# An expert layer with its gather and spread moved from DMA onto TensorE in a decoder kernel on one core

## Chip, cores and metric

One Trainium2 chip, one core. The metric is the device time of one execution in microseconds (us), all data in float32.

## What is computed

The reference runs one decoder layer over 256 tokens with 16 learned meta tokens in front (272 rows of width D = 2048). A combined input projection feeds three mixers (HGRN2, mLSTM, Mamba-2), an output projection `w_out` (2048 x 2048) adds their result to the residual `h`, and then comes the part that matters here:

```python
u = rmsnorm(h, norm_ffn_w)                        # rows of 2048
g = softmax(u @ w_group + b_group)                # 4 groups, the best one is taken
e = (u @ w_router[group] + b_router[group])       # 8 experts of that group, the best two are taken
out[t] = sum over the two: weight * (silu(u[t] @ w1[e]) * (u[t] @ w3[e])) @ w2[e]
result = rmsnorm(h + out, final_norm_w)[:, 16:]   # the meta rows are dropped
```

There are 32 experts; `w1` and `w3` are 2048 x 512, `w2` is 512 x 2048, so an expert has 3 x 4.19 MB and all of them 402.7 MB. Of the 272 rows each picks two experts, 17 rows to an expert on average. With the reference's inputs the busiest expert gets 28.

## The kernel before

**Projections.** `ring` is a buffer of six slots of 2 MB. The input projection (52 column tiles of 128) and the output projection (16 tiles, u = 52 to 67) stream their weights in chunks of two tiles, chunk c into slot c % 2 (SyncE, L435). A chunk is asked for when all tiles of chunk c - 2 are finished (`in_tile`). In the output projection TensorE computes each tile as 16 matmuls over all 272 rows (`mixed`, L1278 to L1284); a float32 matmul is two instructions in the trace. The first four tiles are computed in three parts each (L1491 to L1507), since their inputs are finished one group after the other (`hg_gated`, `z_done`, `norm_done`). VectorE adds each tile to `hT` (L1171), the residual with features on the partitions. ScalarE squares it (L782) and scales it by the norm weight (L783).

**Routing.** After the last tile TensorE computes the logits (L1519), the sums of squares (L1524) and turns the normalised rows to token order (L1537), and ScalarE writes them to DRAM (`tokens_normed`, L800). VectorE picks groups and experts (`routing`, L284 to L376): up to `chosen` (L327) it finds who goes where; TensorE ranks the rows of each expert (L1541 to L1546); then six rounds with a matmul each (L1551) make, for every expert, the list of its rows, as indices for an indirect DMA. Last, `hT` is turned to token order (L1561) for the final sum.

**Experts.** A pass handles up to 64 rows of one expert (`CAP` = 64); experts with more rows would get further passes, their number is read from `ov_n`. GpSimd gathers the rows from DRAM by an indirect DMA (`gather`, L539), TensorE turns them (L1569), and for `w1` and `w3` runs 32 matmuls of 64 columns by 512 (`up`, L1573): `w1` is used on PSUM partitions 0 to 63 and `w3` on 64 to 127, so that two column groups of the array are in use at a time. ScalarE copies the hidden rows out (L820), TensorE turns them (L1590), ScalarE and VectorE gate them, TensorE runs 16 matmuls for `w2` (`down`, L1593), both halves of D side by side in the array. ScalarE and VectorE weight the result (L830, L1192), and GpSimd scatters it to DRAM (`expert_rows`, `scatter`, L550).

**Order.** Each engine has its program written out by hand. On TensorE an iteration is: up(i), turn rows of i + 1, down(i - 1), turn hidden of i (L1619 to L1623). SyncE loads an expert's weights as six transfers of 2 MB, each into a slot of the ring once the matmuls that read the slot last are done (L446, L456, L459, L472). The four transfers of `w1` and `w3` of expert 0 go out behind the last chunk of `w_out`, the two of `w2` when `w_out` is finished (`in_ev`).

**End.** After the last scatter the rows come back from DRAM (L488), VectorE adds them to `h2` in four additions (L1222, L1224), then come the sum of squares, the root (through Ln and Exp, with table loads), the scaling (L1228) and the transfer out (L491).

Of the kernel before, what the change touches and what calls it, by code (L numbers as in the profile page):

```python
# [28 lines left out]
def hymba_moe_layer(nc, x, meta_tokens, hg_lb_logits, norm_mix_w, w_in, hg_norm_w, ml_b_i, ml_b_f,  # L29
# [4 lines left out]
    i32 = mybir.dt.int32  # L34
# [23 lines left out]
    CAP = 64  # L58
    NB = -(-T // CAP)
    NOV = (2 * T) // (CAP + 1)  # L60
    NC_ = NB * NE

# [31 lines left out]
    with ctx:  # L94
# [6 lines left out]
        ring = sb("ring", [P, NSLOT * SLOT])  # L101
        hT = sb("hT", [P, KD, T])
        uT = sb("uT", [P, KD, T])
        proj = sb("proj", [P, NP_, T])
        pflat = proj[:, :, :].rearrange("p a t -> p (a t)")
# [49 lines left out]
        fss = sb("fss", [P, 2])  # L155
        frs = sb("frs", [P, 2])
# [24 lines left out]
        moff = [0]  # L181

        def mo(n):
            moff[0] += n
            assert moff[0] <= NP_ * T
            return pflat[:, moff[0] - n:moff[0]]


        sqk = proj[:, X0:X0 + 8, :]
        sqa = proj[:, B0, :]  # L190
        lgT = proj[:, B0 + 1, :]
        u2 = mo(NT * D).rearrange("p (a d) -> p a d", a=NT)
        h2 = pflat[:, 0:2 * D].rearrange("p (a d) -> p a d", a=2)
        xs = mo(1024)
        xsT = mo(1024).rearrange("p (c h s) -> p c h s", c=8, h=2)
        hs = mo(512)
        ssb = mo(KF * CAP).rearrange("p (k s) -> p k s", k=KF)
        hTb = mo(KF * CAP).rearrange("p (k s) -> p k s", k=KF)
        ysb = mo(1024)
        fw = uT[:, 0:8, :].rearrange("p k t -> p (k t)")[:, 0:D]  # L200
        hid_ps = pb[3][:, :].rearrange("p (k c) -> p k c", k=KF)

        rat = [moff[0]]

        def ro(n):
            rat[0] += n
            assert rat[0] <= NP_ * T
            return pflat[:, rat[0] - n:rat[0]]

        idx_base = sb("idx_base", [P, 3, NC_])  # L210
        idx_x = sb("idx_x", [P, NC_], i32)
        idx_y = sb("idx_y", [P, NC_], i32)
        ov_x = sb("ov_x", [P, NOV], i32)
        ov_y = sb("ov_y", [P, NOV], i32)
        ov_w = sb("ov_w", [P, NOV])
        ov_e = sb("ov_e", [P, NOV], i32)
        ov_n = sb("ov_n", [P, 1], i32)
        xcol = sb("xcol", [P, 1], i32)
        ycol = sb("ycol", [P, 1], i32)

        u2d = nc.dram_tensor("tokens_normed", (2 * T, 1024), f32, kind="Internal").ap()
        yd = nc.dram_tensor("expert_rows", (4 * T, 1024), f32, kind="Internal").ap()
# [12 lines left out]
            "lg_T rs2 iotas gmax pairs ranks gmax_e rhs_used rhs_ready idx_ready ov_ready gatew_in "  # L235
            "par_in routerw_in in_a in_b in_ev h_ps y_ps y_out f_done out_sem pool_steps "
            "ident_ready consts pool_waited xT_ps col_x xs_in col_y y_act y_dve ys_out y_free "
            "u2_out act_steps conv_done params_zeroed rms_ready gate_cols_in lb_diff lb_exp "
            "alog_exp gf_ready gcols_ready li_ready fd_x fd_tanh fd_e em_t em_exp in_tile conv_acc "
            "xv_T xv_ev e_ready e_exp sq_ready sum_ready rs_ready ssm_gated hsig hg_gate hlin hln z_gate "  # L240
            "hv_T hv_ev lv_d lv_e ml_e ml_exp ml_o ml_abs ml_h mo_gate hg_done sq_acc sq2 "
            "u2T_ready sum2 t_ps t_ev h2_ps h2_ev fw_in xT_ev h_ev hT_ps silu_ev f_sum f_rs "
            "dve_steps x_T x_ev par_T par_ev diag_ready R_ready uT_ready g_rows g_col g_colev "
            "cb_ready cb_ev bc_ready y_ready pt_ready y_ev lv_ps lv_w lvd_ps lv_ev ho_ps ho_ev "
            "ml_ps ml_pt norm_done lg_ready row_ps row_ev hlin_q hg_gated z_done lg_ev xT_ev2 hT_ready"
# [6 lines left out]


        LG = GRP + NE
        io_e = ro(NE)
        io_s = ro(P)
        io_t = ro(2 * NT).rearrange("p (a j) -> p a j", j=2)
        io_c = ro(NC_ - NE)
# [25 lines left out]
        def routing(dve, V, step):  # L284
# [14 lines left out]
            for a in range(NT):  # L299
                last = V.max(mg[:, a, :], g8[:, a, :])  # L300
# [1362 lines left out]
```

## Time and profile before

| | |
|---|---|
| median of 3 runs | 1681.1 us (1680.99 to 1681.78) |
| the profiled execution | 1683.12 us, its span 1681.4 us |
| TensorE matmul busy | 1452.1 us, 86% of the span |
| VectorE, ScalarE, GpSimd busy | 285.2, 250.5, 88.9 us |
| granted TensorE clock, mean | 0.928 of full |
| read from HBM | 498.79 MB, mean 309 GB/s with the 21.10 MB written |

The page slices the span into 40 parts of 42 us; a matmul's busy time includes its way through the array, so a busy TensorE need not be at its peak. The span runs from the first to the last instruction; the device time lies 1.7 us above it.

### The profile page before, as it was taken

To read this page: it belongs to the slowest core of one execution; us is meant where nothing else is said; L and a number is where in the kernel's file an instruction comes from. 1 tells how busy PE (TensorE), PEld (TensorE's weight loads), DVE (VectorE), ACT (ScalarE), POOL (GpSimd) and SP (SyncE) were. 2 spreads that over 40 slices of the span, in tenths; PEclk is the share of its full clock that TensorE was granted. 3 is DMA by queue.
4 is the path that set the end of the run, shared out by engine and by line. 5 is a ranking of instruction groups with operands and counts; after the bars stand their busy time and mean duration, and the time that the engine had idled before them with its cause. 6 is when DMAs were issued, how large, how long until landed. Compare 5 with 4: busy or idle time off the path is not lost.

```text
span 1681.4 us, 16119 instructions
## 1 busy us (share of the span) xinstructions
PE 1452.1 (86%) x6416; PEld 806.2 (48%) x6416; DVE 285.2 (17%) x714; ACT 250.5 (15%) x396; POOL 88.9 (5%) x172
## 2 busy tenths in 40 slices
PE   6999999999998997888878888788788788887881
PEld 3888888777886784433323323223233232232230
DVE  4312542341211014121000000000000000000003
ACT  2112413112150012210000100000001001000002
POOL 2000000000000000010000100100000001000000
PEclk9999999999999999898989989989889899898896
DMA  6343354334332565699999999999999999999994
GB/s 160 100 150 100 101 130 128 101 101 133 118 100 86 164 241 213 248 426 427 428 427 426 427 425 423 423 411 412 424 414 417 424 416 425 418 414 421 415 409 171
DMA packets 125982, 495.83 MB, mean 295 GB/s; under 512 B 27988, under 2 KB 97752, under 8 KB 99928
## 3 DMA queue, kind: packets, MB, share of 16 engines
q1 hardware_dynamic: 115536, 482.98, 72.4%
q0 software_dynamic: 9216, 8.94, 1.5%
q10 hardware_dynamic: 1192, 3.37, 0.6%
q8 instruction: 27, 0.44, 0.1%
q14 instruction: 11, 0.09, 0.0%
HBM read 498.79 MB, written 21.10 MB: 309 GB/s over the span
## 4 chain that ended last, share of the span: by engine, by line
PE 57%; DMA 39%; DVE 1%; ACT 1%; SPq 1%; issue 1%; POOLq 0%; ACTq 0%; DVEq 0%
DMA ring<-in_moe_w_dram 37%; PE bank L1239 24%; PE bank L1582 18%; PE bank L1282 7%; PE bank L1321 1%; DMA ring<-in_w_out_dram 1%; PE bank L1299 1%; PE bank L1250 1%; SPq L446 1%; PE bank L1293 1%; PE bank L1603 1%; PE bank L1267 1%; DMA ring<-in_x_dram 1%; PE bank L1371 1%; PE bank L1519 0%
## 5 line engine op out<-in xcount | busy, mean ns | idle before, releaser
L1582 PE MATMUL bank<-ring,proj 128*64 128x512 f32 x2048 | 530.4, 677 | 160.4 <-DMA ring<-in_moe_w_dram 159.5
L1582 PEld LDWEIGHTS bank<-ring,proj 128*64 128x64 f32 x2048 | 183.0, 156 | 487.1 <-issue 486.0
L1239 PE MATMUL bank<-uT,ring 128*128 128x272 f32 x1664 | 390.3, 394 | 0.0
L1239 PEld LDWEIGHTS bank<-uT,ring 128*128 128x128 f32 x1664 | 313.5, 190 | 64.4 <-issue 1.5
L1603 PE MATMUL bank<-ring,proj 128*64 128x512 f32 x1024 | 227.0, 595 | 1.3 <-DVE proj L1187 0.9
L1603 PEld LDWEIGHTS bank<-ring,proj 128*64 128x64 f32 x1024 | 71.1, 137 | 135.0 <-issue 132.3
L1182 DVE COPY proj<-bank 128x512 f32<-128x512 f32 x32 | 22.1, 692 | 665.4 <-PE bank L1569 665.4
L820 ACT ACTIVATE proj<-bank 128x512 f32<-128x512 f32 x32 | 34.5, 1079 | 674.2 <-PE bank L1582 674.2
L1282 PE MATMUL bank<-proj,ring 128*128 128x272 f32 x512 | 122.8, 404 | 9.2 <-DMA ring<-in_w_out_dram 9.2
L1282 PEld LDWEIGHTS bank<-proj,ring 128*128 128x128 f32 x512 | 100.4, 197 | 31.4 <-DMA ring<-in_w_out_dram 10.0
L640 ACT ACTIVATE proj<-bank 128x272 f32<-128x272 f32 x52 | 20.7, 397 | 296.1 <-PE bank L1239 296.1
L1192 DVE TENSOR_SCALAR proj<-bank,idx_base 128x512 f32<-128x512 f32 x32 | 24.0, 751 | 228.1 <-PE bank L1603 228.1
L830 ACT ACTIVATE proj<-bank,idx_base 128x512 f32<-128x512 f32 x32 | 22.0, 687 | 210.1 <-PE bank L1603 210.1
L557 POOL DMA_INDIRECT expert_rows<-proj,ycol x32 | 32.5, 1015 | 221.7 <-DVE proj L1192 203.6
L543 POOL COPY xcol<-idx_x 128x1 int32 (+1 forms) x32 | 5.8, 183 | 661.9 <-PE bank L1569 630.6
L1569 PEld LDWEIGHTS bank<-ident,proj 128*128 128x128 f32 x256 | 27.4, 141 | 26.3 <-issue 26.3
L1569 PE MATMUL bank<-ident,proj 128*128 128x128 f32 x256 | 34.9, 280 | 1.0 <-ACT proj L809 1.0
L546 POOL DMA_INDIRECT proj<-tokens_normed,xcol x32 | 33.3, 1041 | 25.7 <-POOL xcol L543 25.7
L523 POOL IOTA proj<- 128x32 f32 x1 | 0.2, 158 | 628.7 <-DVE hT L1171 628.7
L1590 PEld LDWEIGHTS bank<-ident,proj 128*128 128x128 f32 x128 | 13.4, 140 | 25.5 <-issue 25.1
L1171 DVE TENSOR_TENSOR hT<-hT,bank 128x272 f32 x16 | 7.0, 438 | 106.9 <-PE bank L1282 106.9
L782 ACT ACTIVATE proj<-hT 128x272 f32<-128x272 f32 x16 | 6.9, 430 | 119.3 <-DVE hT L1171 119.3
(294 smaller groups left out, 706.4 us busy)
## 6 DMA issues: line engine op xcount, KB each, us to landing
ring<-in_moe_w_dram SPq DMA_DIRECT2D x192, 2048.0 KB, 20.3
ring<-in_w_in_dram SPq DMA_DIRECT2D x26, 2048.0 KB, 8.2
ring<-in_w_out_dram SPq DMA_DIRECT2D x8, 2048.0 KB, 8.1
ring<-expert_rows SPq DMA_DIRECT2D x4, 1024.0 KB, 8.2
tokens_normed<-proj ACTq DMA_DIRECT2D x2, 1024.0 KB, 3.9
out_dram<-ring SPq DMA_DIRECT2D x2, 1024.0 KB, 3.9
ring<-in_x_dram SPq DMA_DIRECT2D x1, 1024.0 KB, 8.3
uT<-in_final_norm_w_dram ACTq DMA_DIRECT2D x1, 1024.0 KB, 4.6
```

The lines of the kernel that those rows point to most:

```text
L546: V.indirect_dma_start(out=xs, out_offset=None, in_=u2d[:, :], in_offset=bass.IndirectOffsetOnAxis(ap=xcol[:, 0:1], axis=0), bounds_check= ...
L557: V.indirect_dma_start(out=yd[:, :], out_offset=bass.IndirectOffsetOnAxis(ap=ycol[:, 0:1], axis=0), in_=ysb, in_offset=None, bounds_check= ...
L640: V.activation(proj[:, TILES[u], :], pb[u % 4][:, 0:T], func).then_inc(s["in_ev"], 1)
L820: V.activation(hs.rearrange("t (j k p) -> t j p k", j=2, k=2), pb[2][:, :].rearrange("t (j p k) -> t j p k", j=2, k=2), ACT.Copy).then_inc ...
L830: V.activation(ysb[:, 0:512], pb[4][:, :], ACT.Copy, scale=wcol).then_inc(s["y_act"], 1)
L1182: V.tensor_copy(xsT[:, 4:8, :, :].rearrange("p c h s -> p (c h s)"), pb[1][:, :]).then_inc(s["xT_ev2"], 1)
L1192: V.tensor_scalar(ysb[:, 512:1024], pb[5][:, :], wcol, None, ALU.mult).then_inc(s["y_dve"], 1)
L1239: last = V.matmul(outs, a, b, start=start and j == 0, stop=stop and j == n - 1)
L1282: last = V.matmul(pb[u % 4][:, 0:T], wchunk(c % 2)[:, k, u % 2 * P:(u % 2 + 1) * P], proj[:, MIXED[k], :], start=k == 0, stop=k == 7)
L1569: last = V.transpose(pb[c // 4][:, (c % 4) * P:(c % 4 + 1) * P], xs[:, c * P:(c + 1) * P], ident[:, :])
L1582: last = V.matmul(pb[2][64 * g:64 * g + 64, :], xsT[:, c, part, :], w[:, c, :], start=part + c == 0, stop=part == 1 and c == 7)
L1603: last = V.matmul(pb[4 + d][64 * g:64 * g + 64, :], hTb[:, k, :], w[:, k % 2, g * 1024 + d * 512:g * 1024 + (d + 1) * 512], start=k == 0, ...
```

## The change

The routing covers the 256 real tokens only. A pass has 32 places (`CAP` = 32) and four column groups (`QR` = 4): group g computes the quarter g of the contraction (for `w1`, `w3`) or of D (for `w2`). Gather and scatter through DRAM are gone. For a pass, VectorE makes a one-hot matrix from ranks (`tokens_hot`), TensorE multiplies it with the token rows `u2` (`tokens`), ScalarE copies out, TensorE turns. The four partial hidden results are summed by the product with `selq` in `turn_hidden`. The expert's output is spread back to the token rows by 8 matmuls of 32 rows of contraction each (`combine`), with weighted one-hot matrices turned by `spread`, and VectorE adds each of the 8 to `h2` (`sums`). The weights go into four slots of 4 MB, one matrix each, in two transfers; the logits, the squares and the turn to token order are made tile by tile in the output projection (`by_rows`), which now covers 256 columns. Its first two tiles, not four, are made in parts. The final norm works on pieces of 512 as they come.

```diff
-    CAP = 64
+    NA = SEQ // P
+    CAP = 32
+    QR = P // CAP
+        E_AT = (2 * SLOT, 4 * SLOT, 0, RING + KD * T)
+        def halves(j, e, r):
+            if r < 2:
+                v = (moe_w1, moe_w3)[r][0, bass.ds(e, 1), :, :].rearrange("e (p h k) f -> p h (e k f)", p=P, h=2)
+            else:
+                v = moe_w2[0, bass.ds(e, 1), :, :].rearrange("e (p h k) d -> p h (e k d)", p=P, h=2)
+            return [(eslot(j)[:, h * SLOT:(h + 1) * SLOT], v[:, h, :]) for h in range(2)]
...
+                if 2 * c == NIN + 2:
+                    sp.wait_ge(s["norm_done"], 1)
+                    for dst, src in halves(0, 0, 0):
+                        sp.dma_start(dst, src).then_inc(m_in[0], 16)
+                if 2 * c == NIN + 6:
+                    for dst, src in halves(1, 0, 1):
+                        sp.dma_start(dst, src).then_inc(m_in[1], 16)
+            sp.wait_ge(s["in_tile"], NIN + NOUT)
+            for dst, src in halves(2, 0, 2):
+                sp.dma_start(dst, src).then_inc(m_in[2], 16)
+            sp.wait_ge(s["t_ps"], 4 * NA)
+            sp.wait_ge(s["lg_ready"], 1)
+            for dst, src in halves(3, 1, 0):
+                sp.dma_start(dst, src).then_inc(m_in[3], 16)
+            used = (s["h1_ps"], s["h3_ps"], s["y_ps"])
+            for m in range(4, 16):
+                sp.wait_ge(used[(m - 4) % 3], (m - 4) // 3 + 1)
+                for dst, src in halves(m % 4, m // 3, m % 3):
+                    sp.dma_start(dst, src).then_inc(m_in[m % 4], 16)
...
+            for g in range(4):
+                for a in range(NA):
+                    pool.wait_ge(s["t_ev"], NA * g + a + 1)
+                    V.tensor_tensor(u2[:, a, :].rearrange("t (c p) -> t c p", p=P)[:, :, 32 * g:32 * (g + 1)],
+                                    h2[:, a, g * 512:(g + 1) * 512].rearrange("t (q c) -> t c q", c=16),
+                                    nwrow[:, g * 512:(g + 1) * 512].rearrange("t (q c) -> t c q", c=16),
+                                    ALU.mult).then_inc(s["u2_ev"], 1)
...
+            act.wait_ge(s["ov_ready"], 1)
+            act.dma_start(fw, final_norm_w.partition_broadcast(P)).then_inc(s["fw_in"], 16)
...
+            def sums(n, first=False):
+                for j in range(8):
+                    a, d = j // 4, j % 4
+                    dve.wait_ge(s["cb_ps"], n * 8 + (j + 1))
+                    V.tensor_tensor(h2[:, a, d * 512:(d + 1) * 512], h2[:, a, d * 512:(d + 1) * 512],
+                                    pb[6 + j % 2][:, :], ALU.add).then_inc(s["y_acc"], 1)
...
-                    last = V.matmul(pb[u % 4][:, 0:T], wchunk(c % 2)[:, k, u % 2 * P:(u % 2 + 1) * P],
-                                    proj[:, MIXED[k], :], start=k == 0, stop=k == 7)
+                    last = V.matmul(pb[u % 4][:, 0:SEQ], wchunk(c % 2)[:, k, u % 2 * P:(u % 2 + 1) * P],
+                                    proj[:, MIXED[k], NM:T], start=k == 0, stop=k == 7)
...
+            def by_rows(k):
+                pe.wait_ge(s["in_ev"], 4 + NIN + k + 1)
+                if k % 4 == 0 and k:
+                    pe.wait_ge(s["t_ev"], NA * (k // 4))
+                for a in range(NA):
+                    last = V.transpose(pb[5 + a][:, (k % 4) * P:(k % 4 + 1) * P],
+                                       hT[:, k, NM + a * P:NM + (a + 1) * P], ident[:, :])
+                    if k % 4 == 3:
+                        last.then_inc(s["t_ps"], 1)
+                for a in range(NA):
+                    last = V.matmul(pb[(4, 7)[a]][:, 0:LG], hT[:, k, NM + a * P:NM + (a + 1) * P], wr[:, k, :],
+                                    start=k == 0, stop=k == KD - 1)
+            def tokens(n):
+                pe.wait_ge(s["oh_ready"], n + 1)
+                for a in range(NA):
+                    for g in range(QR):
+                        last = V.matmul(pb[0][CAP * g:CAP * (g + 1), :], oh[:, a, :], u2[:, a, g * 512:(g + 1) * 512],
+                                        start=a == 0, stop=a == NA - 1)
+            def up(n, slots, counts):
+                pe.wait_ge(s["xT_ev"], n + 1)
+                for r in range(2):
+                    pe.wait_ge(m_in[slots[r]], counts[r])
+                    w = eslot(slots[r]).rearrange("p (k f) -> p k f", f=FE)
+                    for j in range(4):
+                        for g in range(QR):
+                            last = V.matmul(pb[2 + r][CAP * g:CAP * (g + 1), :], xsT[:, j, g, :], w[:, 4 * g + j, :],
+                                            start=j == 0, stop=j == 3)
+                    last.then_inc((s["h1_ps"], s["h3_ps"])[r], 1)
+            def turn_hidden(n):
+                for r, hs in ((0, hs1), (1, hs3)):
+                    pe.wait_ge((s["h1_ev"], s["h3_ev"])[r], n + 1)
+                    for k in range(KF):
+                        last = V.matmul(pb[4][:, (r * KF + k) * CAP:(r * KF + k + 1) * CAP], hs[:, k * P:(k + 1) * P],
+                                        selq[:, :], start=True, stop=True)
+            def down(n, slot_, count):
+                pe.wait_ge(s["hT_ready"], n + 1)
+                pe.wait_ge(m_in[slot_], count)
+                for k in range(KF):
+                    for g in range(QR):
+                        last = V.matmul(pb[5][CAP * g:CAP * (g + 1), :], hTb[:, k * CAP:(k + 1) * CAP],
+                                        w[:, k, g * 512:(g + 1) * 512], start=k == 0, stop=k == KF - 1)
+            def combine(n, first=False):
+                for j in range(8):
+                    a, g = j // 4, j % 4
+                    if not first or j >= 2:
+                        pe.wait_ge(s["y_acc"], n * 8 + (j - 1))
+                    V.matmul(pb[6 + j % 2][:, :], wT[CAP * g:CAP * (g + 1), a * P:(a + 1) * P],
+                             ysb[CAP * g:CAP * (g + 1), :], start=True, stop=True).then_inc(s["cb_ps"], 1)
+            def one(n, at, last=False, first=False):
+                up(n, [at[0][0], at[1][0]], [at[0][1], at[1][1]])
+                if not last:
+                    tokens(n + 1)
+                turn_hidden(n)
+                if not last:
+                    turn_tokens(n + 1)
+                if not first:
+                    combine(n - 1)
+                spread(n)
+                down(n, *at[2])
```

## Rows read from the trace of the kernel before

**Rows 1.** The page: tenths in 40 slices, and one DMA queue (packets, MB, share)

```profile
PEclk9999999999999999898989989989889899898896
DMA  6343354334332565699999999999999999999994
GB/s 160 100 150 100 101 130 128 101 101 133 118 100 86 164 241 213 248 426 427 428 427 426 427 425 423 423 411 412 424 414 417 424 416 425 418 414 421 415 409 171
...
q0 software_dynamic: 9216, 8.94, 1.5%
```

**Rows 2.** Windows: length, then busy us of PE, PEld, DVE, ACT, POOL, clock, DMA share, GB/s

```profile
640.00:680.00 40.00, 30.09 (x148) 18.84 (x145) 18.29 (x95) 15.60 (x28) 2.83 (x7) 0.83 0.43 164
...
750.00:780.00 30.00, 24.96 (x114) 9.45 (x112) 4.76 (x21) 2.57 (x4) 2.45 (x4) 0.94 1.01 427
...
1110.00:1140.00 30.00, 24.75 (x106) 9.15 (x107) 1.86 (x3) 2.52 (x4) 2.44 (x4) 0.89 0.98 408
```

**Rows 3.** The chain that ended last, in one expert: start, us, what

```profile
796.36 20.17 DMA ring<-in_moe_w_dram
816.52 0.14 issue
816.66 9.78 PE bank L1582 x31
```

**Rows 4.** The expert weights' transfers: one line's issues, then SyncE's timeline (start, us)

```profile
L456 SPq MOVE ring<-in_moe_w_dram x30: 29/29/37, 724.2 to 1607.5; - x30
...
610.09 3.30 SPq L446 DMA_DIRECT2D ring<-in_moe_w_dram  x4
...
689.40 0.80 SPq L446 DMA_DIRECT2D ring<-in_moe_w_dram  x2
```

**Rows 5.** Timeline of the output projection: start, us, then idle time before and its releaser

```profile
507.04 3.83 PE L1282 MATMUL bank<-proj,ring 128*128 128x272 f32 x16
507.24 102.81 SPq L435 DMA_DIRECT2D ring<-in_w_out_dram  x7
...
507.67 1.50 DVE L1162 TENSOR_TENSOR proj<-proj,ring 128x272 f32<-128x272 f32 x4 [1.36 <-ACT proj L640]
...
515.55 28.99 PE L1282 MATMUL bank<-proj,ring 128*128 128x272 f32 x112 [4.67 <-DMA ring<-in_w_out_dram]
...
549.03 89.95 PE L1282 MATMUL bank<-proj,ring 128*128 128x272 f32 x384 [4.50 <-DMA ring<-in_w_out_dram]
```

**Rows 6.** Timeline of the routing: start, us, then idle time before

```profile
649.19 0.57 DVE L294 SCALAR_TENSOR_TENSOR proj<-bank,rs,brow 128x36 f32<-128x36 f32 x3 [1.99 <-ACT rs L789]
...
653.82 0.26 DVE L327 TENSOR_TENSOR proj<-proj 128x96 f32<-128x96 f32 x1
...
655.92 0.97 PE L1239 MATMUL bank<-proj,ones 128*128 128x32 f32 x6
...
682.32 10.09 PE L1582 MATMUL bank<-ring,proj 128*64 128x512 f32 x46 [0.83 <-ACT proj L815]
```

**Rows 7.** Groups by shape: count, busy us and mean ns, idle before and releaser

```profile
L1192 DVE TENSOR_SCALAR proj<-bank,idx_base 128x512 f32<-128x512 f32 x32 | 24.0, 751 | 228.1 <-PE bank L1603 228.1
...
L815 ACT ACTIVATE proj<-bank 128x512 f32<-128x512 f32 x32 | 19.1, 597 | 1.4 <-PE bank L1569 1.4
...
L820 ACT ACTIVATE proj<-bank 128x512 f32<-128x512 f32 x32 | 34.5, 1079 | 674.2 <-PE bank L1582 674.2
```

**Rows 8.** Timeline of TensorE inside one expert

```profile
1072.15 7.09 PE L1582 MATMUL bank<-ring,proj 128*64 128x512 f32 x32 [1.99 <-DMA ring<-in_moe_w_dram]
...
1078.18 0.17 PEld L1582 LDWEIGHTS bank<-ring,proj 128*64 128x64 f32 x2 [0.26 <-issue]
1079.17 0.85 PEld L1569 LDWEIGHTS bank<-ident,proj 128*128 128x128 f32 x8 [0.81 <-issue]
```

**Rows 9.** The chain that ended last, its last part: start, us, what

```profile
1625.51 19.70 DMA ring<-in_moe_w_dram
...
1650.59 2.64 DMA expert_rows<-proj,ycol
```

**Rows 10.** Timeline of the end

```profile
1662.20 2.29 DVE L1224 TENSOR_TENSOR proj<-proj,ring 128x2048 f32<-128x2048 f32 x1 [0.21 <-DMA ring<-expert_rows]
...
1672.15 5.27 SPq L491 DMA_DIRECT2D out_dram<-ring  x2
```

More of the change, by code:

```diff
@@ L473, in _ @@
+            for m in range(88, 3 * NE):
+                sp.wait_ge(used[(m - 4) % 3], (m - 4) // 3 + 1)
+                for dst, src in halves(m % 4, m // 3, m % 3):
+                    sp.dma_start(dst, src).then_inc(m_in[m % 4], 16)
+            sp.wait_ge(s["y_ps"], NE - 1)
             sp.wait_ge(s["ov_ready"], 1)
@@ L862, in _ @@
+            for a in range(NA):
+                act.wait_ge(s["f_rs"], a + 1)
+                act.wait_ge(s["f_g"], 4 * a + 2)
+                V.activation(fout[:, a, 0:1024], fout[:, a, 0:1024], ACT.Copy, scale=frs[:, a:a + 1]).then_inc(
+                    s["f_act"], 1)
         @block.vector
@@ new lines, in _ @@
+            by_rows(NOUT - 1)
+            pe.wait_ge(s["pairs"], 1)
+            for a in range(NA):
+                product(pb[7][:, a * NE:(a + 1) * NE],
+                        [(ones[:, 0:P], chosen[:, j, :]) for j in range(a)] + [(before[:, :], chosen[:, a, :])])
+            product(pb[7][:, NA * NE:(NA + 1) * NE],
+                    [(ones[:, 0:P], chosen[:, a, :]) for a in range(NA)]).then_inc(s["ranks"], 1)
+            def tokens(n):
+                pe.wait_ge(s["oh_ready"], n + 1)
+                for a in range(NA):
+                    for g in range(QR):
+                        last = V.matmul(pb[0][CAP * g:CAP * (g + 1), :], oh[:, a, :], u2[:, a, g * 512:(g + 1) * 512],
+                                        start=a == 0, stop=a == NA - 1)
+                last.then_inc(s["xs_ps"], 1)
@@ new lines, in _ @@
+            pe.wait_ge(s["u2_ev"], 4 * NA)
+            tokens(0)
+            turn_tokens(0)
+            one(0, places(0), first=True)
+            up(1, [places(1)[0][0], places(1)[1][0]], [places(1)[0][1], places(1)[1][1]])
+            tokens(2)
+            turn_hidden(1)
+            turn_tokens(2)
+            combine(0, first=True)
+            spread(1)
+            down(1, *places(1)[2])
+            for n in (2, 3, 4):
+                one(n, places(n))
+            with pe.Fori(1, 7) as i:
+                for q in range(1, 5):
+                    one(i * 4 + q, [(j, i * 96 + c) for j, c in places(q)])
@@ L1628, in _ @@
+            for n in range(29, NE):
+                one(n, places(n), last=n == NE - 1)
             pe.wait_ge(s["ov_ready"], 1)
             count = pe.value_load(ov_n[0:1, 0:1], min_val=0, max_val=NOV)
+            combine(NE - 1)
             with pe.If(count > 0):
                 with pe.Fori(0, count) as i:
-                    turn_rows(i + NE)
-                    up(i + NE, (1, 0))
+                    tokens(i + NE)
+                    turn_tokens(i + NE)
+                    up(i + NE, [0, 1], [i * 32 + (32 * (3 * NE // 4) + 32)] * 2)
```

773 lines of the change are left out of this document (312 added, 461 removed).

## Prediction, made before the changed kernel was run

> **What bounds the kernel now.** The page first: from the eighteenth slice to the last but one the DMA row reads 9 and the traffic 411 to 428 GB/s, where the mixers moved 86 to 248 [rows 1]. The windows confirm it: DMA share 1.01, TensorE busy 24.96 of 30 us [rows 2]. The chain of waits then shows one pattern per expert: a transfer of 20.17 us, 9.78 us of matmuls of L1582, and the next transfer [rows 3]. A transfer of 2 MB takes that long because it stands behind others, so the chain's matmul pieces are no second bound: transfers queue without a hole. From 724.2 to 1607.5 us the first slot of `w2` was refilled 30 times, so an expert takes 883.3 / 29 = 30.46 us [rows 4]. It moves 12.58 MB of weights and 8.94 / 32 = 0.28 MB of gathered and scattered rows [rows 1], together 422 GB/s. The transfers of expert 0 are the only ones made ahead; the next is issued at 689.40 [rows 4], 50.4 us after the last matmul of `w_out` (549.03 + 89.95 = 638.98) [rows 5]. Six transfers of about 5 us each cannot fill that, and the window of the routing shows a DMA share of 0.43 [rows 2]. The last weights land at 1625.51 + 19.70 = 1645.2 [rows 9], and 36.2 us of end follow. The span is thus 638.98 + 50.4 + 955.8 + 36.2 = 1681.4 us.
>
> **The change, part by part.** I build its span anew and compare it with 1681.4.
>
> *Output projection.* 384 instructions of 272 columns take 89.95 us, 0.234 us each [rows 5]; with 256 columns 0.2205, a tile of 32 takes 7.06 us. Sixteen take 113.0 us from 507.04. The pieces of 4 tiles made TensorE wait 4.67 and 4.50 us for chunks 27 and 28 [rows 5]. Now two tiles fill the time from 507.04 to 521.2. Chunk 27 lands at about 515.5, chunk 28 is asked for at 521.2 behind the first 4 MB of expert 0, issued when the group norm ends at 509.2 (507.67 + 1.50) [rows 5], and lands before 530, needed at 536. Both stalls go, and what comes late next is nothing, since a chunk is used in 15 us and a 4 MB transfer with a chunk behind takes about 18, with one chunk of slack. `by_rows` adds 2 turns and 4 short matmul instructions per tile. Eight weight loads of 128 columns take 0.85 us, 0.106 each [rows 8]; by that 0.64 us a tile, bounded from above by 0.2 each. Fourteen lie before the last tile's end: 9.0 us. The end E is 507.04 + 113.0 + 9.0 = 629.0. ScalarE's squares and copies (4 of about 0.6 to 0.8 us for each fourth tile), VectorE's scaling of `wr` (about 1 us, after 509.2, needed at 521) and the first GpSimd multiplies lie beside the tiles; their cover is over 28 us per four tiles.
>
> *Routing.* After E: addition 0.6, `by_rows` 1.0, two squares 1.6, sum, root and reciprocal 0.9, choosing 4.5 (649.19 to 654.08 for three row tiles), ranks 1.5, last small steps 1.0 [rows 6], tokens 2.1, copy 0.8, turn 0.7, copy 0.8 [rows 7]: `up` of expert 0 starts at E + 15.5, against 682.32 - 638.98 = 43.3 now [rows 6]. GpSimd's last two multiplies must be done by E + 11. VectorE adds 2048 elements of two inputs in 2.29 us [rows 10], 0.57 for 512; GpSimd may be three times slower and still has 3 us for each.
>
> *When DMA runs dry.* Two matrices have landed by E; the third goes out at E + 0.2, the fourth at E + 1.6. Chunk 27, alone, came 8.3 us after its issue (507.24 to 515.55) [rows 5] against 5 us in the stream, so 3.3 us of start. Both are in at E + 23. The first slot is freed by the first half of `up`, at E + 19.0, at half clock E + 22.5. So the hole of the routing closes; I take 0 and keep 0 to 5.
>
> *The stream.* From E on, 94 matrices of 4.194 MB. At 422 GB/s each takes 9.93 us: 933.4 us. A stretch without the GpSimd queue isn't in the trace; the best window is 427, one without disturbance on it was 408, though the gathers were alike in both [rows 2]. So I credit the missing 0.28 MB and nothing more; 427 gives 923, 408 gives 966. The final norm's weights, 1 MB across all partitions, now go out beside the last `w2`: 2.5 us. The last weights land at D = 629.0 + 0.2 + 3.3 + 933.4 + 2.5 = 1568.4.
>
> *TensorE must keep up*: 29.8 us per expert. Two column groups give 7.09 / 32 = 0.222 us per instruction of 512 columns [rows 8]; one would give 0.2342 x 512 / 272 = 0.441 [rows 5], so two ran side by side in full. With four I take p = 0.111 for the 64 + 16 + 32 instructions of `up`, `tokens` and `down`: 12.4 us; the upper bound is 0.222. `combine` has two banks: matmul 0.88, hand-over 0.3 to 0.4, addition 0.75 [rows 7], two in flight: 1.0 each, 8.0 us. Turns: 22 loads of 0.106, 2.3 us. At a change from column groups to the whole array the next loads come 0.99 us after the last pair's, which otherwise follow each other by 0.43 [rows 8]: 0.56 us, four times 2.2. Sum 24.9, and up to 2.7 more at the half clock after an idle stretch (9.78 against 7.09) [rows 3, 8]: 27.6. It fits, hidden behind the transfers. VectorE has some 9.5 us per expert (8 additions of 0.75), ScalarE 3.5. Four slots of 4 MB let a matrix be used up to 29 us after it landed before SyncE's next wait starves the queue; the matrix of `w2` is used about 10 us late.
>
> In the Trainium skill, TensorE: Matmul & The Clock Gate, the section on measured speedup gives 3.07 for four row tiles rather than 4. By that p would be 0.139 and the sum 28.0, still under 29.8. The Trainium skill's TensorEngine Tiling, Key Properties, says that changing the tiling mode drains TensorE, which the 0.56 us bears out; it asks for no other number.
>
> *The end.* `w3` of expert 31 is in 12.4 us before D. Half an `up` 3.5, copy and turn 2.3, `combine` of expert 30 8.0, spread 0.8: `down` starts at D + 2.1, ends D + 5.9. Copy 0.8, `combine` 8.6, then norm 3 and 1 for GpSimd's lag (no row shows its multiply): D + 19.3. The 512 KB out take about 3.5; now 1 MB leaves at 1677.1 and ends at 1681.4 [rows 10]. Scatter (2.64 us) [rows 9], read-back, the long additions and the table loads in between are gone. End: 22.8 against 36.2.
>
> **Sum.** 1568.4 + 22.8 = 1591.2, 90.2 under 1681.4. The profiled execution is at 1683.12, 2.0 above the median of 1681.1, so the median becomes 1681.1 - 90.2 = 1590.9. By parts: output projection -10.0, from there to the start of the stream -46.9 (50.4 to 3.5), more weights after it but faster ones -19.9 (955.8 to 935.9), end -13.4.
>
> **Rivals.**
> - *TensorE becomes the bound, slower.* Four column groups give no more than two. For: every instruction of L1582 and L1603 uses two, no row uses four. Against: two scaled fully. With p = 0.222 an expert takes 37.3 us; from 644.5 on 32 of them and 17 us give 1855. It is slower than now above 31.9 us an expert, which is p above 0.173.
> - *TensorE is the bound, but mildly*, p 0.155 to 0.173, or `combine` handing over more slowly: 30 to 31.9 us an expert, 1605 to 1675, say 1650. The margin of 2 to 5 us speaks for it.
> - *The routing still leaves the DMA dry*, as it does now: the first slot free at E + 50, 27 us of hole: 1618. GpSimd's multiplies or a wait chain I read too kindly would do it.
> - *The weights come at 408 GB/s throughout*, since a matrix is now read in strides of 32 KB: 1624.
> - *It doesn't do what it says*: with 32 places instead of 64 there are further passes, over 30 us each. The busiest expert has 28 rows, so none.
>
> **Chances.** Forecast 0.73; mildly bound 0.08; dry start 0.07; slow weights 0.05; slower 0.06; further passes 0.01. The range 1573 (427 GB/s and an end 6 us shorter) to 1625 holds the forecast, the dry start and the slow weights. About 0.2% is what a measurement can tell from no change. Faster 0.93, same 0.01, slower 0.06.
>
> **What would show it.** Right: `up` of expert 0 at 640 to 650, no window after 630 with a DMA share under 0.95, refills of one slot 39.7 us apart (four matrices), `up` in about 7 us for 64 instructions, 20 to 25 us from the last landing to the end. Wrong: in the chain, `combine` or L1582's successor without transfers between; `up` at 14 us; a hole in DMA before 680.

## The result and the profile after

The changed kernel takes 1595.8 us (1590.2 to 1596.0, 4 runs) against 1681.2 for the kernel before on the same chip: a ratio of 0.948, 95% interval 0.946 to 0.950. The forecast was 1591 with a range of 1573 to 1625. The profiled execution has a span of 1593.7 us, 87.7 under the 1681.4 of before.

The page of the changed kernel, to be read beside [rows 1]: the span, TensorE, then clock, DMA share and traffic in 40 slices of 40 us.

```profile
span 1593.7 us, 18575 instructions
...
PE 1461.9 (92%) x7715; PEld 793.2 (50%) x7715; DVE 448.8 (28%) x1033; ACT 314.2 (20%) x470; POOL 36.5 (2%) x59
...
PEclk9999999999999999878867878778778778788786
DMA  6335253333444833899999999999999999999992
GB/s 169 106 106 159 84 135 106 106 106 106 130 134 165 316 127 144 359 428 426 428 428 428 428 428 429 429 428 428 428 429 428 428 429 429 428 428 428 429 426 112
```

The weights are still what the time waits for: the DMA row has a 9 in every slice from the eighteenth to the last but one, and the traffic there is now an even 426 to 429 GB/s where before had 409 to 428. The queue of the indirect DMAs is gone from the page. The clock row is new: mostly 7 and 8 where before had 8 and 9.

Windows of the changed kernel (columns as in [rows 2]):

```profile
630.00:660.00 30.00, 20.02 (x122) 7.74 (x122) 11.28 (x48) 6.98 (x11) 3.76 (x2) 0.66 0.81 338
...
648.00:650.00 2.00, 2.00 (x16) 0.52 (x12) 0.00 (x0) 0.32 (x1) 0.00 (x0) 0.50 0.31 131
650.00:652.00 2.00, 2.00 (x12) 0.39 (x8) 0.00 (x0) 0.00 (x0) 0.00 (x0) 0.50 0.00 0
652.00:654.00 2.00, 2.00 (x20) 0.56 (x16) 0.00 (x0) 0.32 (x1) 0.00 (x0) 0.76 0.00 0
654.00:656.00 2.00, 2.00 (x24) 0.48 (x16) 0.00 (x0) 0.28 (x1) 0.00 (x0) 1.00 0.79 197
...
1110.00:1140.00 30.00, 26.15 (x162) 9.27 (x158) 7.51 (x15) 5.23 (x7) 0.00 (x0) 0.83 1.01 428
```

A hole is left in the transfers, from 648.6 to 654.4. By the DMA shares it is 2 x 0.69 + 4 + 2 x 0.21 = 5.8 us. After it there is none, and TensorE has under 4 us of 30 to spare. At 428 GB/s a matrix of 4.194 MB takes 9.80 us.

The timeline from the last tile of the output projection to the first refill, against [rows 5, 6]:

```profile
620.55 7.15 PE L1256 MATMUL bank<-big 128*128 128x256 f32 x32
...
637.40 0.63 PE L1213 MATMUL bank<-big,before 128*128 128x32 f32 x2 [8.37 <-DVE big L322]
...
640.92 3.64 PE L1516 MATMUL bank<-big 128*32 128x512 f32 x16 [1.18 <-DVE big L1100]
...
645.27 1.12 PE L1523 MATMUL bank<-ident,big 128*128 128x128 f32 x4 [0.71 <-ACT big L729]
...
647.07 9.97 PE L1533 MATMUL bank<-big 128*32 128x512 f32 x64 [0.69 <-ACT big L733]
...
653.68 4.24 SPq L426 DMA_DIRECT2D big<-in_moe_w_dram  x4
```

The projection ends at E = 627.70 (620.55 + 7.15), both of its stalls are gone, and `up` of expert 0 starts at E + 19.4. TensorE was idle for 8.4 us ahead of the ranks and stays at half clock until 653. So the first half of `up` takes 6.6 us instead of 3.64.

One expert inside the loop on TensorE, against [rows 8]; L1533 is `up`, L1568 `combine`, L1557 `down`:

```profile
991.65 3.64 PE L1533 MATMUL bank<-big 128*32 128x512 f32 x32 [2.69 <-DMA big<-in_moe_w_dram]
995.10 1.90 PE L1516 MATMUL bank<-big 128*32 128x512 f32 x16
...
999.31 1.13 PE L1568 MATMUL bank<-big 32*128 32x512 f32 x4
1001.21 2.67 PE L1568 MATMUL bank<-big 32*128 32x512 f32 x4 [0.77 <-DVE big L1127]
...
1010.12 5.92 PE L1557 MATMUL bank<-big 128*32 128x512 f32 x32
1015.87 3.61 PE L1533 MATMUL bank<-big 128*32 128x512 f32 x32
```

Four column groups run side by side in full: 3.64 / 32 = 0.114 us per instruction of 512 columns. In `combine` two matmuls lie on different row groups and share their time (their four instructions take 1.13 us together), then wait for VectorE. From the second pair on a pair takes 2.67 us. The windows show a clock of 0.50 from 1002 until about 1014, so `down` takes 5.92 us for as many instructions as `up` runs in 3.6.

The timeline of the end, against [rows 9, 10]. The traffic into the chip's buffers ends at D = 1560.4, by the windows; as in the prediction, the 1 MB of the final norm's weights is part of it:

```profile
1549.57 3.64 PE L1533 MATMUL bank<-big 128*32 128x512 f32 x32 [0.77 <-DMA big<-in_moe_w_dram]
...
1557.01 8.37 PE L1568 MATMUL bank<-big 32*128 32x512 f32 x12 [0.84 <-DVE big L1127]
...
1565.93 6.20 PE L1557 MATMUL bank<-big 128*32 128x512 f32 x32
...
1574.85 10.30 POOL L514 TENSOR_TENSOR big<-big 128x512 f32<-128x512 f32 x8 [940.16 <-DVE big L1127]
...
1586.82 2.88 SPq L451 DMA_DIRECT2D out_dram<-big  x4
```

`down` of the last expert starts 5.5 us after D, when its weights are there, because `combine` of expert 30 stands ahead of it at half clock. The end takes 33.3 us.

**Where the 87.7 us came from.** Output projection 638.98 to 627.70: 11.3. From there to the stream: 50.4, now the hole of 5.8 and a remainder of 3.2, which I put down to the queue's starts and its last, partly filled microseconds: 41.4. The weights after it: 955.8, now 94 x 9.80 + 2.5 = 923.7: 32.1. The end, 36.2 to 33.3: 2.9.

### The profile page after: what moved, and what is told of

The parts are those of the page before. It is cut to its first block, busy times and chain, and to the rows that moved or that the text cites. A ratio compares the mean times of both kernels' runs of the same rounds, so it can differ in the third digit from the quotient of the medians.

```text
span 1593.7 us, 18575 instructions
## 1 busy us (share of the span) xinstructions
PE 1461.9 (92%) x7715; PEld 793.2 (50%) x7715; DVE 448.8 (28%) x1033; ACT 314.2 (20%) x470; POOL 36.5 (2%) x59
## 4 chain that ended last, share of the span: by engine, by line
PE 66%; DMA 29%; DVE 2%; ACT 1%; issue 1%; SPq 0%; ACTq 0%; DVEq 0%
DMA big<-in_moe_w_dram 29%; PE bank L1213 25%; PE bank L1568 9%; PE bank L1533 8%; PE bank L1256 7%; PE bank L1557 6%; PE bank L1516 2%; PE bank L1541 2%; DVE big L1127 1%; PE bank L1295 1%; PE bank L1273 1%; PE bank L1224 1%; PE bank L1267 1%; PE bank L1241 1%; PE bank L1548 1%; DMA big<-in_x_dram 1%
## 5 line engine op out<-in xcount | busy, mean ns | idle before, releaser
L1213 PE MATMUL bank<-big 128*128 128x272 f32 x1664 | 390.3, 394 | 0.0
L1213 PEld LDWEIGHTS bank<-big 128*128 128x128 f32 x1664 | 313.3, 190 | 64.6 <-issue 1.5
L1568 PE MATMUL bank<-big 32*128 32x512 f32 x512 | 278.7, 917 | 32.4 <-DVE big L1127 31.6
L1533 PE MATMUL bank<-big 128*32 128x512 f32 x2048 | 243.4, 619 | 61.6 <-DMA big<-in_moe_w_dram 60.9
L1127 DVE TENSOR_TENSOR big<-big,bank 128x512 f32<-128x512 f32 x256 | 169.1, 686 | 162.0 <-PE bank L1568 160.9
L1557 PE MATMUL bank<-big 128*32 128x512 f32 x1024 | 180.7, 870 | 0.0
L1533 PEld LDWEIGHTS bank<-big 128*32 128x32 f32 x2048 | 62.7, 114 | 236.2 <-issue 147.8
L1568 PEld LDWEIGHTS bank<-big 32*128 32x128 f32 x512 | 92.8, 247 | 174.0 <-DVE big L1127 164.1
L1256 PE MATMUL bank<-big 128*128 128x256 f32 x512 | 113.9, 381 | 0.0
L1256 PEld LDWEIGHTS bank<-big 128*128 128x128 f32 x512 | 96.3, 190 | 12.6
L1557 PEld LDWEIGHTS bank<-big 128*32 128x32 f32 x1024 | 40.0, 153 | 122.1 <-issue 121.9
L1541 PEld LDWEIGHTS bank<-selq,big 128*128 128x128 f32 x512 | 59.6, 191 | 26.8 <-issue 26.8
L1516 PE MATMUL bank<-big 128*32 128x512 f32 x512 | 62.4, 607 | 1.2 <-DVE big L1100 1.2
L1541 PE MATMUL bank<-selq,big 128*128 128x32 f32 x512 | 63.1, 277 | 0.0
L1516 PEld LDWEIGHTS bank<-big 128*32 128x32 f32 x512 | 16.5, 111 | 40.2 <-issue 40.2
```

Of the source, the lines that this page charges most:

```text
L1127: V.tensor_tensor(h2[:, a, d * 512:(d + 1) * 512], h2[:, a, d * 512:(d + 1) * 512], pb[6 + j % 2][:, :], ALU.add).then_inc(s["y_acc"], 1)
L1213: last = V.matmul(outs, a, b, start=start and j == 0, stop=stop and j == n - 1)
L1256: last = V.matmul(pb[u % 4][:, 0:SEQ], wchunk(c % 2)[:, k, u % 2 * P:(u % 2 + 1) * P], proj[:, MIXED[k], NM:T], start=k == 0, stop=k == 7)
L1516: last = V.matmul(pb[0][CAP * g:CAP * (g + 1), :], oh[:, a, :], u2[:, a, g * 512:(g + 1) * 512], start=a == 0, stop=a == NA - 1)
L1533: last = V.matmul(pb[2 + r][CAP * g:CAP * (g + 1), :], xsT[:, j, g, :], w[:, 4 * g + j, :], start=j == 0, stop=j == 3)
L1541: last = V.matmul(pb[4][:, (r * KF + k) * CAP:(r * KF + k + 1) * CAP], hs[:, k * P:(k + 1) * P], selq[:, :], start=True, stop=True)
```

## Experiments

In each, theory A is the one that I held, and the others are its rivals. Where no interval is given there was one run. The experiments ran on several chips, on which the kernel before took 1681.0 to 1683.4 us, and the changed kernel's own nine times lie between 1590.2 and 1596.2. So a difference of some us from 1595.8 means little by itself, and the profiles have to show where it arises.

**The half clock of the routing.** 23 spare matmuls into an unused bank where TensorE would idle:

```diff
+            def fill(n):
+                for _ in range(n):
+                    V.matmul(pb[1][:, 0:SEQ], ident[:, :], ones[:, 0:SEQ], start=True, stop=True)
+            fill(18)
```

(and 3, 1 and 1 more around `tokens` and `turn_tokens` of expert 0)

> The changed kernel with 23 spare matmuls of 256 columns on TensorE, put where it waits between the last row step of the output projection and the first expert. In the changed kernel the granted clock is 0.50 from 632 to 653 us, the first half of expert 0's up takes 6.6 us, the first refill of a slot goes out at 653.68, and no DMA runs for some 6 us before it. Theory A (the half clock makes the hole): clock 1.00 until 650, tokens of expert 0 in 1.8 us rather than 3.67, first refill at 646 to 648, no hole, total 5 to 6 us less, about 1590. Rival B (the hole is made by VectorE's chain and the copies): first refill within 2 us of 653.7, total within 1 us of the changed kernel.

1589.4 us (1589.2 to 1590.2), ratio 0.945 [0.944, 0.946], 6.4 under the changed kernel. Its window, `up` of expert 0 and its first refill:

```profile
630.00:660.00 30.00, 28.96 (x220) 15.41 (x223) 16.15 (x68) 9.40 (x14) 3.88 (x2) 1.00 0.99 416
```

```profile
643.70 7.07 PE L1538 MATMUL bank<-big 128*32 128x512 f32 x64 [0.25 <-ACT big L733]
...
647.40 4.24 SPq L426 DMA_DIRECT2D big<-in_moe_w_dram  x4
```

The clock is full, the refill comes 6.3 us earlier, and the hole is gone but for 0.4 us (a DMA share of 0.81 from 648 to 650). The span falls by as much, from 1593.7 to 1587.4: theory A.

**The half clock of the loop.** `combine` over all 128 rows, so that it adds all four quarters; what it sums is not the layer's output.

```diff
-                    V.matmul(pb[6 + j % 2][:, :], wT[CAP * g:CAP * (g + 1), a * P:(a + 1) * P],
-                             ysb[CAP * g:CAP * (g + 1), :], start=True, stop=True)
+                    V.matmul(pb[6 + j % 2][:, :], wT[:, a * P:(a + 1) * P],
+                             ysb[:, :], start=True, stop=True)
```

> The changed kernel with combine's 8 matmuls taken over all 128 rows of ysb and wT in place of 32 rows; it leaves out the choice of a quarter, so the output is another sum. In the changed kernel the clock drops to 0.50 about 2 us into combine and stays there through down. Theory A (matmuls that use a quarter of the array's rows let the clock fall): clock near 1.00 in combine and down, down in 3.6 us rather than 5 to 6, mean clock over 0.90, the end (last DMA to the end of the span) 6 to 10 us shorter, total 6 to 10 us less. Rival B (the waits between the matmuls, for VectorE's additions, let it fall): clock, down and total unchanged within 1 us.

1590.4 us (1586.3 to 1590.9), ratio 0.945 [0.943, 0.946]: 5.4 less, a little under the 6 to 10 of theory A. On TensorE, in the same expert as above and at the end, and the first refill:

```profile
1001.20 7.60 PE L1568 MATMUL bank<-big 128*128 128x512 f32 x16
...
1008.95 3.64 PE L1557 MATMUL bank<-big 128*32 128x512 f32 x32
...
1564.08 3.64 PE L1557 MATMUL bank<-big 128*32 128x512 f32 x32
1568.44 7.77 PE L1568 MATMUL bank<-big 128*128 128x512 f32 x16 [0.72 <-ACT big L746]
```

```profile
652.83 4.24 SPq L426 DMA_DIRECT2D big<-in_moe_w_dram  x4
```

The clock stays up and `down` takes 3.64 us. The saving is made at the end and not in the routing: with the first refill at 652.83 the span is 1588.3, where a second profile of the changed kernel has the refill at 652.88 and a span of 1593.1.

But two things had changed, the rows and the waits for VectorE: the page's group of this line has 1.1 us of idle time in all, where the changed kernel's has 32.4. So a last experiment kept the 32 rows and was to take the waits away, by issuing every matmul of `combine` twice:

```diff
-                    V.matmul(pb[6 + j % 2][:, :], ...).then_inc(s["cb_ps"], 1)
+                    for _ in range(2):
+                        last = V.matmul(pb[6 + j % 2][:, :], ...)
+                    last.then_inc(s["cb_ps"], 1)
```

> Each of the 8 matmuls of combine is issued twice in a row into the same bank (the second writes the same values again), still over 32 rows. In the changed kernel two of them, on different row groups, run side by side in 1.13 us and TensorE then waits 0.77 us for VectorE's additions; after that the granted clock is 0.50. The run with 128 rows took away both things at once: the few rows, and the waits (1.1 us of idle ahead of that line in the whole run, against 32.4). Theory A, the few rows lower the clock: it falls here too, in spite of TensorE having no waits, a combine takes 12 to 16 us, an expert 31 to 35 us, TensorE becomes the bound and the time is 1650 to 1750. Theory B, the waits lower the clock: a combine takes 8 to 10 us without waits of over 0.2 us, down takes 3.64 again, the granted clock in the window 1110 to 1140 is 0.89 to 0.95, the time 1587 to 1594. If the clock stays up in combine but TensorE still waits, or falls in some experts only, neither is shown.

1694.1 us, 13 more than the kernel before on its chip. From its timeline and its windows:

```profile
1095.27 1.99 PE L1569 MATMUL bank<-big 32*128 32x512 f32 x8
1098.03 12.42 PE L1569 MATMUL bank<-big 32*128 32x512 f32 x24 [0.77 <-DVE big L1127]
```

```profile
1104.00:1106.00 2.00, 2.00 (x5) 0.81 (x3) 0.76 (x2) 0.00 (x0) 0.00 (x0) 0.50 1.11 475
1106.00:1108.00 2.00, 2.00 (x5) 1.31 (x5) 0.62 (x1) 0.00 (x0) 0.00 (x0) 0.50 0.96 410
```

TensorE is busy without a gap for 12.4 us, and the clock stays at 0.50. So 32 rows of contraction hold it down, without any wait: theory A. But the run took away fewer waits than meant. The one after the first pair is left in nearly every expert (28.2 us in all), and the clock falls most often right behind it. That the fall needs no wait either is shown by two experts only. One of them:

```profile
898.39 1.97 PE L1541 MATMUL bank<-selq,big 128*128 128x32 f32 x16
900.19 0.63 PE L1523 MATMUL bank<-ident,big 128*128 128x128 f32 x4
900.76 2.84 PE L1569 MATMUL bank<-big 32*128 32x512 f32 x8
904.36 4.37 PE L1569 MATMUL bank<-big 32*128 32x512 f32 x8 [0.76 <-DVE big L1127]
```

```profile
898.00:900.00 2.00, 2.00 (x23) 1.62 (x15) 0.51 (x2) 1.45 (x2) 0.00 (x0) 1.00 1.01 434
900.00:902.00 2.00, 2.00 (x14) 1.37 (x15) 0.29 (x1) 1.31 (x3) 0.00 (x0) 0.94 0.94 401
902.00:904.00 2.00, 1.60 (x4) 0.02 (x2) 0.39 (x1) 0.00 (x0) 0.00 (x0) 0.50 1.05 451
```

The clock is down before the wait of 0.76 us begins. Nor is a wait of that length enough: in the changed kernel `up` at 991.65 follows an idle time of 2.69 us and takes 3.64 us, at full clock.

An expert of this run takes (1640.3 - 656.9) / 31 = 31.7 us, by the first and the last copy of the hidden rows. In the Trainium skill, TensorE: Matmul & The Clock Gate, the section on a second failure mode puts a clock that swings to short idle times between groups of matmuls that cycle through PSUM banks. `combine` cycles through two banks and has such waits; the rows above show a clock that stays down with none, and in two experts one that falls with none.

**How much TensorE has to spare.** Half the bytes of each expert transfer, from the fifth matrix on; the other half of each slot holds old weights.

```diff
-            return [(eslot(j)[:, h * SLOT:(h + 1) * SLOT], v[:, h, :]) for h in range(2)]
+            n = SLOT if calls[0] <= 4 else SLOT // 2
+            return [(eslot(j)[:, h * SLOT:h * SLOT + n], v[:, h, 0:n]) for h in range(2)]
```

> The changed kernel with only half of each weight transfer behind the first four matrices; the other half of the slot keeps old data, so the output is not the layer's. It measures what TensorE and the others need per expert when the transfers are no bound (a half slot pair is 4.9 us per matrix). Theory A (TensorE has a margin of 2 to 5 us at full clock): 24 to 27 us per expert, total about 1595.7 - 31 x (29.4 - 25.5) = 1475. Rival B (the loop is bound by its own chain near 29 us and the transfers fit by chance): 28.5 to 29.5 us per expert, total over 1565.

1526.0 us: neither theory's total. By the copies of the hidden rows, (1484.6 - 652.2) / 31 = 26.9 us per expert, inside theory A's 24 to 27. TensorE is the bound (28.97 us busy of 30, DMA share 0.58, from 1110 to 1140), and 26.9 is 2.5 under the 3 x 9.80 = 29.4 of the stream. The clock in that window was 0.74.

More work for it, `tokens` issued four times (48 more instructions per expert) and twice (16 more):

```diff
-                for a in range(NA):
+                for a in list(range(NA)) * 4:
```

> The changed kernel with the 16 matmul instructions of tokens made four times for every expert, 48 more of 0.107 us: 5.2 us per expert at full clock; the result stays the same. Theory A (25 to 26 us of work at full clock, and the clock recovers when TensorE no longer pauses): about 30 to 31 us per expert, TensorE bound, total 1610 to 1650. Rival B (more margin than that, work up to 29 us hides): total within 5 us of 1596. Rival C (the clock does not recover): 26.7 + 5.2 or more = 32 to 34 us per expert, total 1675 to 1740.

> The changed kernel with tokens made twice for every expert, 16 more instructions of 0.107 us, 1.7 us of TensorE per expert; the result stays the same. With half the bytes an expert took about 27 us, and with three extra tokens (5.1 us) 32.3. Theory A (TensorE needs 27.2 us at the clock it gets, the queue 29.4): 28.9 us still fits, total within 3 us of 1595.8. Rival B (part of the 2.2 us is needed for waiting on landings, so that every addition shows): 20 to 50 us more.

Four times: 1681.8 us against 1681.6 for the kernel before, at (1640.4 - 659.4) / 31 = 31.6 us per expert and 378 GB/s. Theory A (1610 to 1650) fails here; the total is that of rival C, by which the clock does not recover, though its 32 to 34 us per expert is just missed. Twice: 1594.1 us (1593.0 to 1595.4), ratio 0.947 [0.946, 0.949], no change, as theory A had it. The margin takes 16 instructions, not 48. Break-even lies about where the prediction's rival had put it, at 31.9 us an expert.

**The stream.** The kernel before without its indirect DMAs: gathered rows are then whatever the buffer holds, nothing is scattered, and the final sum reads `x`.

```diff
-                V.indirect_dma_start(out=xs, out_offset=None, in_=u2d[:, :],
-                                     in_offset=bass.IndirectOffsetOnAxis(ap=xcol[:, 0:1], axis=0),
-                                     bounds_check=last_half, oob_is_err=False).then_inc(s["xs_in"], 16)
+                pool.sem_inc(s["xs_in"], 16)
```

(the scatter likewise)

> The kernel before without its 32 gathers and 32 scatters by indirect DMA (each pass computes on what lies in its buffer, and the last additions read x in place of the expert rows; the output is not the layer's). It asks why the weights came at 422 GB/s with the gathers and at 428 in the changed kernel. Theory A (the indirect DMAs cost their bytes and disturb the stream besides): refills of the w2 slot 29.4 us apart, as in the changed kernel, against 30.46; with 29 of them 30 us less, and 3 to 5 us less at the end: about 1645. Rival B (only their bytes, 0.28 MB a pass, 0.65 us): refills 29.8 apart, about 1657. Rival C (the ring of six 2 MB slots costs it, not the gathers): refills over 30.2, over 1668.

1640.9 us (1638.9 to 1641.1) against 1683.4: 0.975 [0.973, 0.976], 42.5 us less. Refills of the first `w2` slot, against [rows 4]:

```profile
L456 SPq MOVE ring<-in_moe_w_dram x30: 29/29/37, 723.4 to 1569.4; - x30
```

846.0 / 29 = 29.17 us per expert instead of 30.46. (By the times at which the transfers landed, from the third expert on, it is 29.37 instead of 30.68: much the same difference, and no faster than the 29.4 of the changed kernel.) The 0.28 MB account for 0.65 of the 1.29 us; the other half is what they cost the stream beside their bytes: theory A. The window of 1110 to 1140, 408 before, reads 428. This one step, done to the kernel before, is worth half of what the whole change is worth (42.5 against 85.4 us).

The order of a matrix in memory, changed to two contiguous halves (rows of the weights then meet other rows of the tokens):

```diff
-                v = ....rearrange("e (p h k) f -> p h (e k f)", p=P, h=2)
+                v = ....rearrange("e (h p k) f -> p h (e k f)", p=P, h=2)
```

> The changed kernel with each half of a matrix read as one contiguous 2 MB, as the kernel before does, in place of 16 KB every 32 KB (the rows of the matrix then meet other rows of the tokens, so the output is not the layer's). Theory A (the order of the 16 KB runs in HBM is nothing to the queue): 9.79 us per matrix, total within 1.5 us of the changed kernel's 1595.8. Rival B (the strided order is what lifts the rate from 422 to 428 GB/s): 9.94 us per matrix, 14 us more, about 1610.

1591.4 us (1590.4 to 1594.9), ratio 0.946 [0.944, 0.948]; 428 to 429 GB/s, as with strides. Rival B falls, but the total is outside theory A's 1.5 us too. The rate does not tell why it was some 4 us less. In its profile the first refill is at 649.26 instead of 653.68, which would be as much. The control asked whether this is a matter of the run, the changed kernel once more:

> The changed kernel once more, on the chip of these runs, to see how far its two groups of times (1590.2 and 1595.8 in the first comparison) belong to the moment at which the clock comes back after the routing. Theory A: its total goes with the first refill's time; a run whose first refill is at 653 to 654 is at 1595 to 1596, one at 649 to 650 is at 1590 to 1592. Rival B: the total differs with the same first refill.

1594.9 us (1591.1 to 1596.2). Over its profile and four others, refill and span go together: 653.68 and 1593.7, 652.88 and 1593.1, 652.56 and 1592.0 (16 more instructions), 649.26 and 1589.3 (layout), 647.40 and 1587.4 (filled). The spread of the changed kernel, 1590 to 1596, would be that too; only profiled executions show a refill, so this is not shown. Why the clock comes back earlier in one execution than in another stays open.

The first two matrices asked for only after `w_out`:

```diff
-                if 2 * c == NIN + 2:
-                    sp.wait_ge(s["norm_done"], 1)
...
             sp.wait_ge(s["in_tile"], NIN + NOUT)
+            sp.wait_ge(s["norm_done"], 1)
+            for dst, src in halves(0, 0, 0):
+                sp.dma_start(dst, src).then_inc(m_in[0], 16)
+            for dst, src in halves(1, 0, 1):
+                sp.dma_start(dst, src).then_inc(m_in[1], 16)
```

> The changed kernel with the first two matrices of expert 0 asked for when the output projection is finished, with the third, in place of during it. Theory A (from the output projection's end on the queue is the bound and the time is the bytes left): 96 matrices instead of 94 behind it, 19.6 us more, less the hole of 6 to 7 us that closes: 1607 to 1610. Rival B (expert 0 starts late and its wait is added whole, since the queue stops too): 1615 or more. Rival C (the first experts hide it): under 1600.

1608.3 us (1607.9 to 1608.7), ratio 0.956 [0.954, 0.957]: 12.5 more. Its window from 630 to 660 shows a DMA share of 1.01, so two matrices more in the stream (19.6) are paid for in part by the hole that they close: theory A, whose 1607 to 1610 holds.

**A better version.** First the spare matmuls, and `combine` over 128 rows with its one-hot matrices masked to the quarter that counts (4 copies by VectorE instead of one), so that it computes what it should:

```diff
-                V.tensor_copy(wT, pb[1][:, 0:NA * P]).then_inc(s["wt_ev"], 1)
+                for g in range(QR):
+                    last = V.tensor_scalar(wT[g], pb[1][:, 0:NA * P], mk[:, g:g + 1], None, ALU.mult)
+                last.then_inc(s["wt_ev"], 1)
```

> The changed kernel with the spare matmuls of e1_fill, and with combine over all 128 rows as in e2_k128, but with the right sums: VectorE writes the spread weights four times, each multiplied by a column that is 1 for one quarter of the partitions and 0 for the others (about 1.3 us more of VectorE per expert, beside TensorE). Theory A (the hole of the routing and the half clock at the end are two separate costs, 6.4 and 5.4 us): total about 1584, first refill at 647 to 648, mean clock over 0.93. Rival B (both runs saved the same thing, the moment at which the clock comes back after the routing): about 1589, as e1_fill.

Then, on top, `combine` of expert 30 between the two halves of `up` of expert 31:

```diff
+                    up(n, *w, (0,))
+                    combine(n - 1)
+                    up(n, *w, (1,))
```

> The kernel of e9_fill_masked with the last expert in another order: combine of expert 30 between the two halves of up of expert 31, while w3 is still on its way, not behind it. Theory A (the end is TensorE's chain behind the last landings, in which 8 us of combine stand for nothing): 2 to 3 us less than e9_fill_masked. Rival B (the last transfer of w2 ends that chain anyway): within 0.7 us of it.

1585.7 us (1585.4 to 1587.2), ratio 0.943 [0.941, 0.944], nearer to theory A's 1584 than to the 1589 of rival B. Then 1579.8 us (1579.2 to 1581.0), 0.939 [0.938, 0.940]: 15 under the changed kernel on the same chip. The reordering, with VectorE's additions moved to match, gave 6 us where I had expected 2 to 3. Its end:

```profile
1546.52 3.64 PE L1542 MATMUL bank<-big 128*32 128x512 f32 x32
...
1553.91 3.64 PE L1566 MATMUL bank<-big 128*32 128x512 f32 x32 [1.59 <-DMA big<-in_moe_w_dram]
1558.25 3.10 PE L1577 MATMUL bank<-big 128*128 128x512 f32 x6 [0.71 <-ACT big L747]
```

Now `down` waits for its weights and not they for it, and 1578.1 - 1553.9 = 24.2 us follow. In the version without the reordering, `up` of `w3` waited 4.92 us for its weights and ran at half clock (6.40 us), and `combine` and `down` came after.

## Why the prediction was right, and where it was not

The time was 1595.8 against a forecast of 1591, in span 1593.7 against 1591.2. The case was the forecast one: the weights' stream is the bound, TensorE keeps up, and the routing no longer holds the stream back for long. But three terms were mis-sized: from E to the stream +5.5, the rate -12.2, the end +10.5. With -1.3 for E they add up to 2.5. That they nearly cancelled is luck; the end alone is off by almost half of its size.

- **Output projection: right.** E 627.70 against 629.0; the turns and short matmuls after each tile took 0.5 us, where 0.64 was taken. Both stalls went.
- **Routing: 3.9 us too short.** `up` started at E + 19.4, not + 15.5. Choosing took 6.7 instead of 4.5 (a copy of 1.80 and a cast of 1.14 us in it), the ranks 2.35 instead of 1.5, `tokens` 3.64 instead of 2.1. The last two are the half clock: in the filled run, where E is 627.28, `up` starts at E + 16.4.
- **"So the hole of the routing closes; I take 0 and keep 0 to 5": wrong by 6.** The first refill came at E + 26.0, past even the E + 22.5 that I had for half clock, and the queue ran dry at E + 20.9 and not at E + 23. I priced the half clock for `up` alone, though the ranks, `tokens` and the turns run at it too. The filled run shows it: full clock, first refill at E + 20.1, a hole of 0.4 us, 6.3 us less.
- **The stream, 9.93 us a matrix: 9.80.** "I credit the missing 0.28 MB and nothing more" was the step that failed. The window at 427 had been nearer than the mean, and the run without indirect DMAs puts the rest on them. Over 94 matrices: 12 us. The strides of 32 KB cost nothing, so the rival with 408 GB/s falls. (The page's traffic before goes down to 409 GB/s, not 411 as I read it; nothing hangs on it.)
- **TensorE must keep up: right, with a thin margin.** p is 0.114 against 0.111, an expert costs 26.9 us against 24.9 to 27.6. The Trainium skill's 3.07, which was put beside the sum and is measured for row tiles, is not what this trace shows for four column groups: 0.441 / 0.114 is 3.9. I had also divided wrongly: 0.441 / 3.07 is 0.144 and not 0.139, which would make the sum 28.6 and not 28.0, still under 29.8. Both rivals of a TensorE bound fall here. Two runs with added work show that such a bound is near, at 31.6 and 31.7 us an expert.
- **The half clock was in the wrong place.** I had it after an idle stretch ("up to 2.7 more"). It comes in every `combine`, about 12 us long, and costs 2.3 us in `down` (5.92 against 3.64) and some in `combine`. In the loop this is hidden behind the weights.
- **The end, 22.8: 33.3.** `down` starts at D + 5.5 instead of 2.1 and takes 6.2 instead of 3.8 (both half clock); from there to the issue of the first transfer out 14.7 instead of 13.4; the transfers out 6.9 instead of 3.5. The last is an error of reading: I scaled one transfer's time, where four are issued over 2.88 us and the last must still land. The run with 128 rows in `combine` has an end of 1588.3 - 1560.1 = 28.2 us. The reordered kernel, at full clock, needs 24.2 us from the start of its last `down`, where the sum had 20.7.
- **Signs named in advance.** `up` of expert 0 at 640 to 650: 647.07. No window under a DMA share of 0.95: one, 0.81. Refills of one slot 39.7 us apart: 4 x 9.80 = 39.2. `up` in about 7 us: 7.3. 20 to 25 us of end: 33. And one sign of being wrong came: a hole in DMA before 680, of 5.8 us, though not the rival's 27.

## What to carry to other kernels

When a transfer-bound stage is moved closer to its bound, its two ends decide: what frees the first slot, and what stands ahead of the last weights' use on the engine that uses them. Price both at TensorE's half clock unless the engine is seen busy with full-height matmuls before; a few spare matmuls, a `combine` over all 128 rows and one reordering were together worth 15 us here. And a small stream of indirect transfers beside a full queue can cost twice its bytes, as it did here (1.29 us against 0.65).

## What the runs showed of the hardware that was not expected

- Float32 matmuls over 32 rows of contraction hold TensorE's clock at 0.50, the lower of its levels (1.2 GHz), even while the engine is busy without a gap for 12.4 us; over 128 rows `combine` and the `down` behind it run at full clock (7.60 and 3.64 us).
- Four column groups of 32 scale fully: 0.114 us per instruction against 0.222 for two.
- Indirect DMAs of 2% of the bytes cost the weights' stream 4% of its time.
- ScalarE now reloads its tables twice per expert, for the copy ahead of Silu and for Silu:

```profile
L742 ACT ACT_TABLE_LOAD x31 | 39.8, 1283 | 0.6
L737 ACT ACT_TABLE_LOAD x31 | 39.8, 1283 | 0.5
```

They take 1.28 us each and are off the path; I had not priced them. In the loop of the kernel before there was none.
